# First mixer of a two-block model: head outputs of two pairs back to back, decays and causal products moved

## The reference

```python
proj = h @ w_in                                   # z, xBC, dt
z, xBC, dt_raw = jnp.split(proj, [D_INNER, D_INNER + CONV_DIM], axis=-1)
xBC = jax.nn.silu(causal_depthwise_conv(xBC, conv_w, conv_b))
dt = jax.nn.softplus(dt_raw + dt_bias)
cum = jnp.cumsum(dt * A, axis=1)
L = jnp.exp(jnp.where(causal, cum[:, :, None] - cum[:, None, :], -jnp.inf))   # decays
CB = jnp.einsum('btgn,bsgn->btsg', C, B)                                     # products of B and C
y = jnp.einsum('btsg,btsgh,bsgh,bsghp->btghp', CB, L, dt, x)                 # head outputs
y = (y + D_skip * x) * jax.nn.silu(z)
y = rms_norm by group of 512 channels, times g_out, then @ w_out
```

## Time and profile before

| | us |
|---|---|
| median of three runs | 1813.01 |
| lowest and highest | 1812.87, 1813.54 |
| span of the profiled execution, first to last instruction | 1810.9 |
| TensorE busy in it | 1799.0 |
| VectorE busy | 1039.5 |
| ScalarE busy | 735.5 |
| first mixer's loop of pairs, heads 0 to heads 15 | 64.7 to 287.6 |

### The profile page before, as it was taken

One profiled execution on the slowest core, in us unless ns is written; L12 is line 12 of the kernel. 1 busy time (PEld: TensorE's weight loads), 2 busy tenths in 40 slices (PEclk: granted clock), 3 DMA queues, 4 the chain that ended last, 5 costly groups with the idle time before them and its releaser, 6 DMA issues.

```text
span 1810.9 us, 21230 instructions
## 1 busy us (share of the span) xinstructions
PE 1799.0 (99%) x8390; PEld 1454.8 (80%) x8390; DVE 1039.5 (57%) x1502; ACT 735.5 (41%) x1202; POOL 71.1 (4%) x137
## 2 busy tenths in 40 slices
PE   9999999999999999999999999999999999999998
PEld 7777777888766788888888888888888888888887
DVE  8899986566687565444333356554444544444333
ACT  5788885433477532322222332223222322322221
POOL 1002021001210000000000000000000000000000
PEclk9999999999999999999999999999999999999999
DMA  5466562232211223333333323233333333323331
GB/s 177 93 108 112 112 107 83 98 93 93 72 36 36 82 81 105 93 93 100 93 100 101 119 81 95 95 95 102 94 98 100 94 93 102 97 93 93 102 99 56
DMA packets 50578, 170.85 MB, mean 94 GB/s; under 512 B 5808, under 2 KB 8368, under 8 KB 50480
## 3 DMA queue, kind: packets, MB, share of 16 engines
q1 hardware_dynamic: 47376, 161.44, 28.5%
q0 software_dynamic: 2240, 7.34, 4.8%
q10 hardware_dynamic: 864, 0.72, 0.1%
HBM read 167.31 MB, written 2.16 MB: 94 GB/s over the span
## 4 chain that ended last, share of the span: by engine, by line
PE 93%; DVE 4%; ACT 1%; issue 1%; DMA 0%; SPq 0%; DVEq 0%; ACTq 0%
PE pb L771 28%; PE pb L773 27%; PE pb L772 27%; PE pb L990 2%; PE pb L882 2%; PE pb L1019 1%; PE pb L995 1%; PE pb L1163 1%; PE pb L1165 1%; PE pb L1164 1%; PE pb L785 1%; DVE CV L1741 0%; DVE wl L1569 0%; PE pb L1173 0%; DMA raw<-in_ssm_in 0%
## 5 line engine op out<-in xcount | busy, mean ns | idle before, releaser
L771 PE MATMUL pb<-XR,wr 128*128 128x512 f32 x1584 | 625.4, 395 | 0.6 <-DVE wl L1569 0.4
L773 PE MATMUL pb<-XR,wl 128*128 128x512 f32 x1584 | 617.0, 390 | 0.0
L772 PE MATMUL pb<-XL,wr 128*128 128x512 f32 x1584 | 616.9, 389 | 0.0
L1569 DVE TENSOR_TENSOR wl<-raw,wr 128x1024 fp32r<-128x1024 f32 (+1 forms) x297 | 358.3, 1206 | 351.0 <-ACT wr L1221 349.9
L1221 ACT ACTIVATE wr<-raw 128x1024 fp32r<-128x1024 f32 (+1 forms) x295 | 305.3, 1035 | 299.1 <-PE pb L773 273.6
L771 PEld LDWEIGHTS pb<-XR,wr 128*128 128x128 f32 x1584 | 297.4, 188 | 65.8 <-issue 3.9
L773 PEld LDWEIGHTS pb<-XR,wl 128*128 128x128 f32 x1584 | 297.2, 188 | 62.6
L772 PEld LDWEIGHTS pb<-XL,wr 128*128 128x128 f32 x1584 | 297.6, 188 | 60.2 <-issue 0.2
L771 PE MATMUL pb<-ffn2HR,wr 128*128 128x512 f32 (+1 forms) x198 | 72.7, 367 | 0.0
L772 PE MATMUL pb<-ffn2HL,wr 128*128 128x512 f32 (+1 forms) x198 | 72.3, 365 | 0.0
L773 PE MATMUL pb<-ffn2HR,wl 128*128 128x512 f32 (+1 forms) x198 | 72.3, 365 | 0.0
(11 more groups left out here) (354 smaller groups left out, 2317.6 us busy)
## 6 DMA issues: line engine op xcount, KB each, us to landing
raw<-in_ffn_in SPq DMA_DIRECT2D x88, 512.0 KB, 3.5
raw<-in_mix_in SPq DMA_DIRECT2D x48, 512.0 KB, 3.5
raw<-in_ssm_in SPq DMA_DIRECT2D x40, 512.0 KB, 4.3
raw<-in_ffn_out SPq DMA_DIRECT2D x32, 512.0 KB, 3.5
DB<-cum POOLq DMA_DIRECT2D x28, 256.0 KB, 8.6
raw<-in_ffn_out SPq DMA_DIRECT2D x16, 384.0 KB, 3.2
raw<-in_mla_in SPq DMA_DIRECT2D x11, 512.0 KB, 3.3
raw<-in_ssm_out_a SPq DMA_DIRECT2D x8, 512.0 KB, 3.2
```

The lines of the kernel that those rows point to most:

```text
L771: e.matmul(o, r, xr, start=first, stop=False)
L772: e.matmul(o, r, xl, start=False, stop=False)
L773: return e.matmul(o, l, xr, start=False, stop=last)
L1569: e.tensor_tensor(wl[j % NS][:, 0:width(j)], raw[j % NR][:, 0:width(j)], wr[j % NS][:, 0:width(j)].bitcast(F32), ALU.subtract).then_inc(s_ ...
```

## The change

Block q of the loop is put in a different order from q = 3, and the outputs of pairs 1 and 2, 3 and 4, up to 13 and 14, stand together at the end of the even block. Before, a block was: product q, tile one, decays q + 1, tile two, output q. After, for q of 3 or more: decays q, tile one, product q, tile two, and in even blocks output q - 1 and output q. Block 1 keeps product 1, tile one, decays 2, tile two; block 2 has product 2, both tiles, outputs 1 and 2. Output 15 comes alone after block 15. Outputs of even pairs from 2 on lie in bank 3 instead of 6. Nothing is added to or taken from the computation.

As `zgate` waits for the output, gates 1 and 3 are done later: gates 1 and 2 both in tile 21 (before, in tiles 20 and 21), gates 3 and 4 both in tile 34 (before, 22 and 34). The norm of group 0 follows two tiles later.

```diff
     for q, (one, two) in enumerate(pair_units(), 1):
-        steps.append(("mul", q))
+        if q > 2:
+            steps.append(("decay", q))
+        else:
+            steps.append(("mul", q))
         unit(one)
+        if q == 1:
+            steps.append(("decay", 2))
         if q == 2:
             conv(19)
             gates.reverse()
-        if q < 15:
-            steps.append(("decay", q + 1))
+        if q > 2:
+            steps.append(("mul", q))
         unit(two)
-        y(q)
+        if q % 2 == 0:
+            y(q - 1)
+            y(q)
+    y(15)
     steps.append(("ysplit", 0))
...
         elif what == "y":
-            bk.place(("y", n), 6, (s_y, n + 1), (s_yn, n + 1))
+            bk.place(("y", n), 6 if n == 0 or n % 2 else 3, (s_y, n + 1), (s_yn, n + 1))
...
                     w.wait_ge(*bk.full["y", n])
-                    e.scalar_tensor_tensor(out=YN[:, n, :], in0=YN[:, n, :], scalar=col("ssm_D", n), in1=PB[6][:, :],
+                    e.scalar_tensor_tensor(out=YN[:, n, :], in0=YN[:, n, :], scalar=col("ssm_D", n), in1=PB[bk.bank["y", n]][:, :],
                                            op0=ALU.mult, op1=ALU.add).then_inc(s_yn, 1)
```

## The result

The changed kernel takes 1827.26 us (1826.43 to 1828.23, 4 runs) against 1813.03 us (1812.87 to 1813.54, 4 runs) of the kernel before: 14.2 us or 0.8% more, ratio 1.008 with a 95% interval of 1.0068 to 1.0091. The span of the profiled execution grew from 1810.9 to 1824.7 us, by 13.8. The four runs of the changed kernel lie in two groups, 1826.43 and 1826.52, 1827.99 and 1828.23; the median stands between them, and the profile is that of the run of 1826.52.

The account below looks back on a forecast made before the run. TensorE, busy 99% of the span, was taken as the bound, with VectorE lacking slack in the first mixer. Losses of 16.1 us less 1.0 of waits and 0.9 of joins gave +14.2 on 1813.0: 1827, range 1817 to 1833.

Parts of the forecast that it names:

- The bound: Whole kernel, chiefly first mixer: TensorE busy 99% of the span; VectorE behind there, so waits in its queue may reach TensorE.
- What it gains: Head blocks: each joined pair saves one exit and one entry, 0.3 us; seven pairs would give 2.1 us.
- Block 2: Tile 3 and outputs 1 and 2: TensorE loses 1.4 us at the B and C products, 0.2 at bank 3.
- Block 3: Fold waits 7.2 us for gate 1's square behind decays 3; TensorE then loses 4.3, 0.2, 1.6 (tok 5) and 4.1 us.
- Blocks 5 to 15: Later blocks: 4.3 us lost in tile 7 and at outputs 8, 12, 14 and 15; pairs 6, 8, 10 gain 0.9.
- Nothing is given back: Stages after the mixer: none can win back the delay, as none has TensorE waiting for something it would hide.
- The clean gain: First rival: buffers absorb VectorE's lag and only the edges remain, 1810.9 us, at best 1808.4; chance 0.08.
- The second: Rival: block 3's fold wait alone costs, the rest absorbed: 1814.4, or 1818 with tok 5 and half of output 4; chance 0.10.
- The third (pairs not back to back): Rival: the second product is late in every even block, 1 to 4 us in seven blocks: +20, 1833; chance 0.08.
- The fourth, the clock: Rival: lower clock behind two waits of about 4 us, up to 5.5 us more each, +11, 1838; chance 0.06.
- Its own signs: Profile after: fold idle some 7 us, waits of about 4 us in tile 4 and heads 3/4, heads 5/6 joined, output 4 near 137.
- wrong if the granted clock falls: A stated failure sign, beside the fold not waiting and heads 3 and 4 touching; granted clock had been 1.00 in both stages.

Follow-up runs that it names:

- the squares first: The changed kernel with the two gate squares of tile 21 ahead of decays 3 on ScalarE instead of behind them: 1822.69 us.
- the kernel with pairs up to 4: The changed kernel with, from block 6 on, the order of the kernel before and single outputs: 1825.62 us.
- the one with single outputs: The changed kernel's order of decays and products, but every output alone at the end of its own block, in bank 6: 1829.44 us.

## Why the prediction was right, point by point

The predicted time, 1827, is the measured one, and the range held it. That it fits to 0.3 us is in part luck: no single run took 1827, the trace gives +13.8 us where the prediction has +14.2, and some of its terms are wrong in opposite directions. By its own steps:

- **The bound.** VectorE without slack, so that a wait in its queue reaches TensorE: right, 6.85 us of VectorE's idle time became 3.82 us of TensorE's, and taking it away gave 4.6 us by the medians, 3.7 by the traces.
- **What it gains.** 0.3 us for each joined pair: measured 0.34. Of the seven pairs I had three joined without a wait (6, 8, 10); it is one, heads 5 and 6. Heads 7 and 8 have a wait of 0.69 us between them, and heads 9 and 10 take 225.89 - 221.11 = 4.78 us, 0.32 too much for a joined pair: VectorE's product 10 ended at 223.4, just when heads 9 were done.
- **Block 2.** 1.4 and 0.2 us: two waits of 0.34 and 0.82 us in tile 3, tile 3 longer by 1.36 us, and 0.23 us at bank 3. Heads 2 end 1.37 us late.
- **Block 3.** The fold at 110.68 for 111.0, tile 4's wait 3.97 us by the pitch for 4.3, product 4 at 131.3 to 134.2 for 131.8 to 134.8, output 4 at 136.74 for 137.3. But two terms are not as I had them. The 1.6 us at tok 5 did not occur. Instead the clock fell behind the wait in tile 4, a slow tok 4 and then matmuls at a pitch of 0.42 us, together 2.6 us, and TensorE came to tok 5's bank only when it was free; with the squares first, where the clock stays up there, 0.7 us of this wait is seen. And the wait between heads 3 and 4 was 3.4 us for 4.1. At heads 4 the terms add up to 10.8 us (the clock readings in the text, 137.3 against 127.1, to 10.2), and 9.7 were measured, for partly another reason.
- **Blocks 5 to 15.** 3.4 us net, by my sum 4.3 - 0.9: measured 4.0. Mis-sized one by one: tile 7 0.3 us for 0.6, heads 8 0.7 for 0.1, heads 10 0.3 for nothing, heads 12 0.9 for 1.0, heads 14 2.3 for 1.7, heads 15 0.3 for 0.9. That they depend on what stands ahead of a z tile's eviction I had; that the norm's scaling is one of these things, and lay well only because gate 3 had become late, I had not seen.
- **Nothing is given back.** Right: 13.7 us at heads 15, 13.8 in the span.
- **The rivals.** The clean gain fell. The second did not hold, as the later waits came too. The third (pairs not back to back) is partly true, for six of seven pairs, but at a lower price. The fourth, the clock, came true at one of the two waits that I named, at 2.6 us for my bound of 5.5, and took the place of the 1.6 us at tok 5; I had given it 0.06 and nothing in the sum. The Trainium skill's warning about idle gaps ("TensorE: Matmul & The Clock Gate", HAM oscillation) is borne out in part: the last section has the waits behind which the clock fell and those behind which it did not.
- **Its own signs.** The fold, the waits, the joined heads 5 and 6 (0.34 us under twice 2.5) and output 4 at 136.7 us came as described, and from heads 8 to heads 15 the loss was 3.7 us, near the 4 of blocks 8 to 15. But "wrong if the granted clock falls" came true too, 0.52 behind the wait in tile 4. The mechanism of waits stands; that a wait costs only itself was wrong.

## What to carry to other kernels

When steps are reordered on engines that walk one list, look first for a short instruction that another engine's short instruction waits for (here a 0.6 us square) and that now stands behind a long group (7.3 us of decays); its wait cost more than all the joins could gain. Joining two head blocks was worth a third of a microsecond, so it pays only where the second block's input comes less than that late: make its inputs early first, and only where the engine that makes them has slack. Look also for what the reordering moves without being asked, as the norm's scaling here, 3.9 us by its place. And a block that is taken away from its place was cover for the waits behind it.

## What the runs showed of the hardware

TensorE's clock can fall to the lower level behind a single short wait in the middle of work that is otherwise dense. Heads that take 2.31 us took 3.53 behind a wait of 2.53 us, 3.67 behind 3.20, 3.42 behind 3.31, 3.90 behind 3.99 and 4.00 behind 5.03, in five of these kernels. The windows view shows the granted clock in the first and the fourth of these stretches, 0.64 and 0.58:

```profile
96.70:100.30 3.60, 3.57 (x17) 1.51 (x17) 3.48 (x5) 3.58 (x10) 1.16 (x2) 0.64 0.49 30
...
129.30:133.30 4.00, 3.97 (x17) 1.99 (x17) 3.86 (x6) 2.49 (x6) 0.00 (x0) 0.58 0.82 95
```

In the change the slow stretch follows a wait of 3.82 us in tile 4, and in the kernel with pairs up to 4 one of 3.83. With the long pitches behind the heads counted in, a fall cost 1.6 to 1.7 us in the five kernels and 2.6 in tile 4 of the change, beside the wait.

Yet 3.35 us in the change, 3.17 us between heads 3 and 4 of the kernel with pairs up to 4, 2.46 us before heads 8 of the one with single outputs, and 2.06 us before tok 5 were followed by matmuls at full pace. So the length of the wait alone does not decide it between 2.5 and 3.4 us; what else does stays open. The two longest without a fall have one thing in common: the clock had already fallen in tile 4 of the same kernels and come back, at about 119 us. Each of these is one execution, and whether the clock falls behind the same wait in every execution no trace here tests.
